# One feed-forward stage of a layer trunk: where VectorE splits the weights of its block products, and where it reads their banks

## The chip, the cores and the metric

The kernel runs on one core of one Trainium2 chip. The metric is the device time of one execution in microseconds; the time of a kernel is the median of its runs. Engines are named as in the profile: PE (TensorE) multiplies, DVE (VectorE) and ACT (ScalarE) work elementwise, POOL (GpSimd) helps and issues some transfers, SP (SyncE) issues the transfers of weights.

## The reference, cut to what matters

Two layers, x of 512 tokens by 1024, in float32. Layer 0 mixes with a recurrent and an RWKV-7 branch, layer 1 with retention; each is followed by a squared-ReLU feed-forward stage, with norms before and after:

```python
def sq_relu_mlp(x, w_in, w_out):
    return jnp.square(jax.nn.relu(x @ w_in)) @ w_out
...
f = sq_relu_mlp(rms_norm(h, norm_ffn_pre[layer]), ffn_w_in[layer], ffn_w_out[layer])
h = h + rms_norm(f, norm_ffn_post[layer])
```

The change lies in the feed-forward stage of layer 1, the last stage: w_in is 1024 by 4096, w_out 4096 by 1024.

## The kernel before, in words

Every product is made of three matmuls in a narrower float format: an operand a is split into a high part (a rounded, written by ACT) and a low part (a minus its high part, written by DVE), and high times high, high times low and low times high are added up in a PSUM bank. Weights come from DRAM in chunks of 128 by 2048 (1 MB) through a ring of three places (`raw`, `WL` over the same bytes, `WH`). SP issues the load of chunk c when PE has begun with chunk c - 2, which shows that it has left c - 3. ACT writes `WH` (L340, or in halves L353 and L354), DVE then writes `WL` (L346, or in halves L359 and L361), and PE waits for `WL` in `chunk_ready`.

The last stage goes over four quarters of the 4096 hidden columns (`ffn_pe`, `ffn_act`, `ffn_dve`). In a quarter whose first chunk is c, eight tiles j = 0 to 7 of hidden activations are computed first, from chunks c to c + 3: PE fills a bank (L388, L391, L394), DVE takes relu (L873) and the square (L881), ACT squares the relu again into the high part AH (L845), DVE subtracts for the low part AL (L884). Chunk c + j/2 + 2 is split by DVE at the end of each even tile (`split_lo`).

In quarters 0, 1 and 2 the second product is computed with seven block products in place of eight (`seven_pe`, `seven_dve`). Of the activations' four blocks four sums are needed (S_both, four steps L747, L748, L750, L752 for each k tile, in `activation_sums`), and of the weights too; the latter were made in an earlier stage and lie in DRAM. Here "sum k" is k tile k of the activations' sums, k = 0 to 3; it is formed behind tile j = 4 + k. Its high part S_high is written by ACT (L708), its low part S_low by DVE (L712, `sums_low`), which stands behind the low part of the next tile, and for sum 3 in `seven_dve`. Product i, i = 0 to 6, uses chunk c + 4 + i and two banks of `SEVEN_BANKS`, each for 128 tokens and 4 k steps: 24 matmuls (L691, L694, L695). Products 0 to 2 use the tiles A themselves, 3 to 6 the sums:

```python
SEVEN_BANKS = ((4, 5), (6, 7), (0, 1), (2, 3), (4, 5), (2, 3), (4, 5))
if t == 0 and i < 2:
    pe.wait_ge(S("a_lo"), done + 4 * i + k + 1)
if t == 0 and i == 3:
    pe.wait_ge(S("sums_lo"), 4 * q + k + 1)
```

So product 1 waits in its k step k for the low part of tile 4 + k, and product 3 for the S_low. DVE adds the two banks of each product into fT (L735, L737), which frees them (`acc_free`). Quarter 3 uses an ordinary product (`out_by_token_pe`), and in quarter 1 PE also turns h by transposes into banks 4 to 7 (L563, `turn_h_pe`), the first of them once banks 4 and 5 are free. POOL loads gain_row (0.5 MB, for the last norm) once the last S_low is written (L1973).

The order of the work is written out by hand: each engine runs its own program, in the order of the loops, and waits on semaphores.

Of the kernel before, what the change touches and what calls it, by code (L numbers as in the profile page):

```python
# [145 lines left out]
def trunk_kernel(nc, x, weights, pairs, vectors, const, ret_const, last_gain, out):  # L146
    with ExitStack() as ctx:
# [5 lines left out]
        def S(name):  # L153
            name = SERIES_OF.get(name, (name,))[0]
            if name not in sems:
                sems[name] = ctx.enter_context(nc.semaphore(name))
            return sems[name]
# [86 lines left out]
        for i in range(2):  # L244
# [5 lines left out]
            q, k = over(f"q{i}", [2, T]), over(f"k{i}", [2, T])  # L250
# [44 lines left out]
        def size(c):  # L295
            return CHUNK // 2 if c in AG_CHUNKS else CHUNK
# [45 lines left out]
        def split_lo(dve, c):  # L342
            if c < ALL_CHUNKS:
                i, n = c % RING, size(c)
                dve.wait_ge(S("w_hi"), c + 1)
                nc.vector.tensor_tensor(WL[i][:, :n], raw[i][:, :n], WH[i][:, :n], ALU.subtract).then_inc(S("w_lo"), 1)  # L346
# [9 lines left out]
        def split_halves_lo(dve, c, n):  # L356
            i, m = c % RING, CHUNK // 2
            dve.wait_ge(S("first_hi"), n + 1)
            nc.vector.tensor_tensor(WL[i][:, :m], raw[i][:, :m], WH[i][:, :m], ALU.subtract)  # L359
            dve.wait_ge(S("w_hi"), c + 1)  # L360
            nc.vector.tensor_tensor(WL[i][:, m:], raw[i][:, m:], WH[i][:, m:], ALU.subtract).then_inc(S("w_lo"), 1)  # L361
# [150 lines left out]
        def post_sum_dve(dve, m, i):  # L512
            dve.wait_ge(S("fsq"), m * KT + 2 * i + 4)
            if i:
                dve.wait_ge(S("fsq_sum_b"), 2 * m + i)
            nc.vector.tensor_tensor(sum_b, sum_b if i else sq[:, 1, :], sq[:, 2 * i + 3, :],
                                    ALU.add).then_inc(S("fsq_sum_b"), 1)
# [28 lines left out]
        def add_to_f(dve, use, b, m, first):  # L546
            n = use.next(b)
            dve.wait_ge(S(f"acc_full{b}"), n)
            if first:
                nc.vector.tensor_copy(f[:, m, :], bank[b][:]).then_inc(S(f"acc_free{b}"), 1)  # L550
            else:
                nc.vector.tensor_tensor(f[:, m, :], f[:, m, :], bank[b][:], ALU.add).then_inc(S(f"acc_free{b}"), 1)  # L552
# [157 lines left out]
        def sums_low(dve, q, k):  # L710
            dve.wait_ge(S("sums_hi"), 4 * q + k + 1)
            nc.vector.tensor_tensor(S_low[:, :, k, :], S_both[:], S_high[:, :, k, :], ALU.subtract).then_inc(S("sums_lo"), 1)  # L712
# [6 lines left out]

        def seven_dve(dve, use, c, q):  # L720
            for i, banks in enumerate(SEVEN_BANKS):
                split_halves_lo(dve, c + 6 + i, 7 * q + i)
                if i == 1:
                    sums_low(dve, q, 3)
                for t, b in enumerate(banks):
                    u = use.next(b)
                    dve.wait_ge(S(f"acc_full{b}"), u)
                    for tokens, outputs, sign in ADDENDS[i]:
                        to = fT[:, 2 * tokens + t, outputs * T:(outputs + 1) * T]
                        last = added.get((tokens, outputs, t))  # L730
                        added[tokens, outputs, t] = b, u
                        if last:
                            dve.wait_ge(S(f"acc_free{last[0]}"), last[1])
                        if not last:
                            ins = nc.vector.tensor_scalar(to, bank[b][:], float(sign), None, ALU.mult)  # L735
                        else:
                            ins = nc.vector.tensor_tensor(to, to, bank[b][:], ALU.add if sign > 0 else ALU.subtract)  # L737
                    ins.then_inc(S(f"acc_free{b}"), 1)

        def activation_sums(dve, q, k):  # L740
            n = 4 * q + k
            dve.wait_ge(S("a_square"), 8 * QUARTERS + 8 * q + 4 + k + 1)
            if n:
                dve.wait_ge(S("sums_lo"), n)
            a11, a21 = first_squared[:, k, 0:HALF], first_squared[:, k, HALF:T]
            a12, a22 = squared[:, k % 2, 0:HALF], squared[:, k % 2, HALF:T]
            nc.vector.tensor_tensor(S_both[:, 0, :], a21, a22, ALU.add).then_inc(S("s_step"), 1)  # L747
            nc.vector.tensor_tensor(S_both[:, 2, :], a11, a21, ALU.subtract).then_inc(S("s_step"), 1)  # L748
            dve.wait_ge(S("s_step"), 4 * n + 1)
            nc.vector.tensor_tensor(S_both[:, 1, :], S_both[:, 0, :], a11, ALU.subtract).then_inc(S("s_step"), 1)  # L750
            dve.wait_ge(S("s_step"), 4 * n + 3)
            nc.vector.tensor_tensor(S_both[:, 3, :], a12, S_both[:, 1, :], ALU.subtract).then_inc(S("s_step"), 1)  # L752
# [35 lines left out]
        def quarter_at(c0, layer, q):  # L788
            return FFN1_AT[q] if layer else c0 + 8 * q
# [71 lines left out]
        def ffn_dve(dve, use, c0, m, layer):  # L861
            dve.wait_ge(S("rb_ready"), m + 1)
            for q in range(QUARTERS):
                done = 8 * QUARTERS * layer + 8 * q
                c = quarter_at(c0, layer, q)
                for j in range(8 if layer else 16):
                    b = j % 4
                    if j < 8:
                        u = use.next(b)
                        dve.wait_ge(S(f"acc_full{b}"), u)  # L870
                        if j >= 2:
                            dve.wait_ge(S("a_lo"), done + j - 1)
                        nc.vector.scalar_tensor_tensor(relu[:, j % 2, :], bank[b][:], 0.0, rB[:], ALU.max,  # L873
                                                       ALU.mult).then_inc(S(f"acc_free{b}"), 1)
                        dve.wait_ge(S(f"acc_free{b}"), u)
                        n, square = T, squared[:, j % 2, :]
                        if layer and q < SEVEN and j < 4:
                            n, square = HALF, first_squared[:, j, :]
                        if layer and q + j // 6:
                            dve.wait_ge(S("s_step"), 16 * min(q, SEVEN) + (4 * (j - 5) if j >= 6 and q < SEVEN else 0))  # L880
                        nc.vector.tensor_tensor(square, relu[:, j % 2, :], relu[:, j % 2, :], ALU.mult).then_inc(S("a_square"), 1)  # L881
                        dve.wait_ge(S("a_square"), done + j + 1)
                        dve.wait_ge(S("a_hi"), done + j + 1)
                        nc.vector.tensor_tensor(AL[:, j, :n], square[:, :n], AH[:, j, :n], ALU.subtract).then_inc(S("a_lo"), 1)  # L884
                        if layer and q < SEVEN and j > 4:
                            sums_low(dve, q, j - 5)
                        if layer and q < SEVEN and j >= 4:
                            activation_sums(dve, q, j - 4)
                    else:
                        add_to_f(dve, use, b, j - 8, q == 0)  # L890
                        if q == QUARTERS - 1 and j in (12, 14):
                            post_sum_dve(dve, m, j // 2 - 6)
                    if j % 2 == 0 and (q or j):
                        split_lo(dve, c + j // 2 + 2)
                    if not layer and q < SEVEN and j in (9, 11, 13, 15):
                        weight_sums_dve(dve, 4 * q + j // 2 - 4)
                if layer and q < SEVEN:
                    seven_dve(dve, use, c, q)
                elif layer:
                    out_by_token_dve(dve, use, c, q)  # L900
# [1146 lines left out]
        def _(dve):  # L2047
# [70 lines left out]
            for m, c0, layer, kind, post, pre in ((1, FFN0_CHUNK, 0, 2, (0, 3), (1, 0)), (2, RET_CHUNK0, 1, 0, (1, 1), (1, 2)),  # L2118
                                                  (3, FFN1_CHUNK, 1, 2, None, None)):
                pre_sums_dve(dve, m)  # L2120
                split_lo(dve, c0 + 2)
                pre_rstd_dve(dve, m)
                if m == 2:
                    ret_dve(dve, use, m)
                else:
                    ffn_dve(dve, use, c0, m, layer)
                if post:
                    residual_dve(dve, m, post, pre)
# [112 lines left out]
```

## Time and profile before

| | |
|---|---|
| median of 3 runs | 1475.59 us (1475.32 to 1476.76) |
| the profiled execution, its own time | 1476.38 us |
| its span | 1474.6 us |
| mean granted clock of PE | 0.986 |
| DVE busy | 921.6 us, 63% |
| ACT busy | 538.2 us, 36% |
| POOL busy | 87.1 us, 6% |
| last stage, quarters 0 to 3 | about 1140 to 1461 us |

The time of an execution is the span and some 2 us around it. A busy share is a mean over all stages; what ends a wait in one stage is read from the rows of that stage. Matmuls are pipelined: each lasts longer than the step from its start to that of the next, so the pace is read from the starts.

### The profile page before, as it was taken

The page shows a single profiled execution, that of the slowest core. Times are in us where ns is not written, and L with a number is a line of the kernel's source. Part 1 is how long each engine was busy: PE and PEld are TensorE (multiplying, and loading weights), DVE is VectorE, ACT ScalarE, POOL GpSimd, SP SyncE. Part 2 cuts the span into 40 slices and gives each one's busy share as a digit, 9 for nine tenths or more (in the row PEclk, how much of TensorE's full clock was granted, in tenths as well). Part 3 has the DMA queues.
Part 4 walks back from the last instruction along what each step waited for, and adds up shares of the span by engine and source line. Part 5 has one row for each costly group of instructions (what it writes and reads, how often), then busy time and mean ns, then how long its engine had stood idle before and what let it go on. Part 6 is the DMA issues. An engine that isn't in the chain of part 4 may idle for free.

```text
span 1474.6 us, 22076 instructions
## 1 busy us (share of the span) xinstructions
PE 1434.8 (97%) x9650; PEld 1181.9 (80%) x9650; DVE 921.6 (63%) x1200; ACT 538.2 (36%) x632; POOL 87.1 (6%) x89
## 2 busy tenths in 40 slices
PE   9999999998999999998999999999998999999997
PEld 6778787777888888887888888888887788888786
DVE  7768676667655565654756445355447876868754
ACT  7555454533312222223343332332434433433322
POOL 0000000012010100001200000000003000000000
PEclk9999999998999999999999999999998999999999
DMA  5211111101474654731222122222130352434332
GB/s 187 73 36 59 50 59 45 59 30 42 178 266 143 224 181 175 263 112 60 86 68 100 62 86 92 81 86 86 62 110 29 132 182 86 171 115 166 134 110 62
DMA packets 30623, 160.21 MB, mean 109 GB/s; under 512 B 2816, under 2 KB 6912, under 8 KB 15552
## 3 DMA queue, kind: packets, MB, share of 16 engines
q1 hardware_dynamic: 23456, 130.73, 25.0%
q0 software_dynamic: 7072, 28.08, 5.4%
q8 instruction: 76, 1.25, 0.3%
q14 instruction: 19, 0.16, 0.0%
HBM read 144.12 MB, written 14.68 MB: 108 GB/s over the span
## 4 chain that ended last, share of the span: by engine, by line
PE 89%; DVE 6%; ACT 2%; issue 1%; DMA 1%; POOL 0%; DVEq 0%; POOLq 0%
PE bank L388 21%; PE bank L394 20%; PE bank L391 20%; PE bank L691 2%; PE bank L695 2%; PE bank L694 2%; PE bank L1681 2%; PE bank L1675 2%; PE bank L1678 2%; PE bank L993 2%; PE bank L402 1%; DMA raw<-weights 1%; PE bank L1000 1%; DVE WL L346 1%; PE bank L593 1%
## 5 line engine op out<-in xcount | busy, mean ns | idle before, releaser
L388 PE MATMUL bank<-XH,WH 128*128 128x512 f32 x944 | 379.4, 402 | 15.4 <-DVE XL L481 12.6
L391 PE MATMUL bank<-XL,WH 128*128 128x512 f32 x944 | 371.2, 393 | 0.0
L394 PE MATMUL bank<-XH,WL 128*128 128x512 f32 x944 | 371.0, 393 | 0.0
L346 DVE TENSOR_TENSOR WL<-raw,WH 128x2048 fp32r<-128x2048 f32 (+1 forms) x99 | 222.1, 2245 | 136.7 <-ACT WH L340 136.6
L340 ACT ACTIVATE WH<-raw 128x2048 fp32r<-128x2048 f32 (+1 forms) x99 | 185.2, 1872 | 189.9 <-DMA raw<-weights 189.8
L388 PEld LDWEIGHTS bank<-XH,WH 128*128 128x128 f32 x944 | 179.5, 190 | 58.8 <-issue 19.5
L394 PEld LDWEIGHTS bank<-XH,WL 128*128 128x128 f32 x944 | 179.4, 190 | 38.7
L391 PEld LDWEIGHTS bank<-XL,WH 128*128 128x128 f32 x944 | 179.7, 190 | 38.2 <-issue 2.1
L845 ACT ACTIVATE AH<-relu 128x512 fp32r<-128x512 f32 (+1 forms) x64 | 37.9, 592 | 216.4 <-DVE relu L873 216.4
L388 PE MATMUL bank<-AH,WH 128*128 128x512 f32 x256 | 99.7, 390 | 0.0
L391 PE MATMUL bank<-AL,WH 128*128 128x512 f32 x256 | 99.6, 389 | 0.0
L394 PE MATMUL bank<-AH,WL 128*128 128x512 f32 x256 | 99.6, 389 | 0.0
L552 DVE TENSOR_TENSOR f<-f,bank 128x512 f32<-128x512 f32 x64 | 43.0, 684 | 67.2 <-PE bank L394 67.0
L873 DVE SCALAR_TENSOR_TENSOR relu<-bank,rB 128x512 f32<-128x512 f32 x64 | 44.0, 688 | 64.9 <-PE bank L394 64.8
L388 PEld LDWEIGHTS bank<-AH,WH 128*128 128x128 f32 x256 | 48.0, 188 | 10.2 <-DVE AL L884 0.3
L394 PEld LDWEIGHTS bank<-AH,WL 128*128 128x128 f32 x256 | 48.0, 188 | 10.0
L391 PEld LDWEIGHTS bank<-AL,WH 128*128 128x128 f32 x256 | 48.0, 188 | 10.0
L388 PE MATMUL bank<-BH,WH 128*128 128x512 f32 x128 | 50.2, 392 | 0.3 <-DVE f L552 0.2
L394 PE MATMUL bank<-BH,WL 128*128 128x512 f32 x128 | 49.8, 389 | 0.0
L391 PE MATMUL bank<-BL,WH 128*128 128x512 f32 x128 | 49.8, 389 | 0.0
L1675 PE MATMUL bank<-WH,XH 128*128 128x512 f32 x128 | 49.8, 389 | 0.0
L1678 PE MATMUL bank<-WL,XH 128*128 128x512 f32 x128 | 49.8, 389 | 0.0
(360 smaller groups left out, 2339.3 us busy)
## 6 DMA issues: line engine op xcount, KB each, us to landing
raw<-weights SPq DMA_DIRECT2D x104, 1024.0 KB, 4.8
block<-weights POOLq DMA_DIRECT2D x12, 1024.0 KB, 7.6
sums_of_blocks<-block POOLq DMA_DIRECT2D x12, 1024.0 KB, 5.3
raw<-sums_of_blocks SPq DMA_DIRECT2D x12, 1024.0 KB, 4.8
raw<-weights SPq DMA_DIRECT2D x8, 512.0 KB, 4.5
h<-x_fm SPq DMA_DIRECT2D x4, 512.0 KB, 8.1
out_tm<-h SPq DMA_DIRECT2D x8, 256.0 KB, 2.6
rc<-ret_const POOLq DMA_DIRECT2D x1, 1536.0 KB, 8.1
```

Of the source, the lines that this page charges most:

```text
L340: nc.scalar.activation(WH[i][:, :n], raw[i][:, :n], ACT.Copy).then_inc(S("w_hi"), 1)
L346: nc.vector.tensor_tensor(WL[i][:, :n], raw[i][:, :n], WH[i][:, :n], ALU.subtract).then_inc(S("w_lo"), 1)
L388: mm = pe.matmul(bank[b][:], wh, xh, start=(k == 0), stop=False)
L391: mm = pe.matmul(bank[b][:], wh, xl, start=False, stop=False)
L394: mm = pe.matmul(bank[b][:], wl, xh, start=False, stop=(k == len(xs) - 1))
L552: nc.vector.tensor_tensor(f[:, m, :], f[:, m, :], bank[b][:], ALU.add).then_inc(S(f"acc_free{b}"), 1)
L691: mm = pe.matmul(bank[b][:], xh, wh, start=(k == 0 and not ADDED[i]), stop=False, skip_group_check=True)
L694: pe.matmul(bank[b][:], xh, wl, start=False, stop=False, skip_group_check=True)
L845: nc.scalar.activation(AH[:, j, :n], relu[:, j % 2, :n], ACT.Square).then_inc(S("a_hi"), 1)
L873: nc.vector.scalar_tensor_tensor(relu[:, j % 2, :], bank[b][:], 0.0, rB[:], ALU.max, ALU.mult).then_inc(S(f"acc_free{b}"), 1)
L1675: mm = pe.matmul(bank[2 + t][:], XH[:, kt, tok], wh, start=(kt == 0), stop=False)
L1678: mm = pe.matmul(bank[2 + t][:], XH[:, kt, tok], wl, start=False, stop=False)
```

## The change

It moves instructions of DVE and changes nothing else. In tile 6 of the last stage's quarters the split of chunk c + 5 (product 1's) is written right behind the tile's low part, ahead of S_low of sum 1 and the steps of sum 2, where it was behind them. In `seven_dve` the two banks of product i are read first, and the split of chunk c + 6 + i (and S_low of sum 3, for i = 1) follows, where the split came first.

```diff
--- before.py
+++ after.py
@@ -719,9 +719,6 @@
 
         def seven_dve(dve, use, c, q):
             for i, banks in enumerate(SEVEN_BANKS):
-                split_halves_lo(dve, c + 6 + i, 7 * q + i)
-                if i == 1:
-                    sums_low(dve, q, 3)
                 for t, b in enumerate(banks):
                     u = use.next(b)
                     dve.wait_ge(S(f"acc_full{b}"), u)
@@ -736,6 +733,9 @@
                         else:
                             ins = nc.vector.tensor_tensor(to, to, bank[b][:], ALU.add if sign > 0 else ALU.subtract)
                     ins.then_inc(S(f"acc_free{b}"), 1)
+                split_halves_lo(dve, c + 6 + i, 7 * q + i)
+                if i == 1:
+                    sums_low(dve, q, 3)
 
         def activation_sums(dve, q, k):
             n = 4 * q + k
@@ -882,6 +882,8 @@
                         dve.wait_ge(S("a_square"), done + j + 1)
                         dve.wait_ge(S("a_hi"), done + j + 1)
                         nc.vector.tensor_tensor(AL[:, j, :n], square[:, :n], AH[:, j, :n], ALU.subtract).then_inc(S("a_lo"), 1)
+                        if layer and j == 6:
+                            split_lo(dve, c + 5)
                         if layer and q < SEVEN and j > 4:
                             sums_low(dve, q, j - 5)
                         if layer and q < SEVEN and j >= 4:
@@ -890,7 +892,7 @@
                         add_to_f(dve, use, b, j - 8, q == 0)
                         if q == QUARTERS - 1 and j in (12, 14):
                             post_sum_dve(dve, m, j // 2 - 6)
-                    if j % 2 == 0 and (q or j):
+                    if j % 2 == 0 and (q or j) and not (layer and j == 6):
                         split_lo(dve, c + j // 2 + 2)
                     if not layer and q < SEVEN and j in (9, 11, 13, 15):
                         weight_sums_dve(dve, 4 * q + j // 2 - 4)
```

DVE's rows of quarter 0 from the low part of tile 6 to the square of tile 7, before. `WL2` is the ring place of product 1's chunk; L747 to L752 are a sum's steps.

```order
L884 TENSOR_TENSOR AL_106<-squared_108,AH_105 128x512
L712 TENSOR_TENSOR S_low_109<-S_both_113,S_high_111 128x4x256
L747 TENSOR_TENSOR S_both_113<-first_squared_112,squared_108 128x256
L748 TENSOR_TENSOR S_both_113<-first_squared_112 128x256
L750 TENSOR_TENSOR S_both_113<-S_both_113,first_squared_112 128x256
L752 TENSOR_TENSOR S_both_113<-squared_108,S_both_113 128x256
L346 TENSOR_TENSOR WL2_57<-raw2_56,WH2_58 128x2048
L873 SCALAR_TENSOR_TENSOR relu_107<-bank2,rB 128x512
L881 TENSOR_TENSOR squared_108<-relu_107 128x512
```

And in the changed kernel:

```order
L884 TENSOR_TENSOR AL_106<-squared_108,AH_105 128x512
L346 TENSOR_TENSOR WL2_57<-raw2_56,WH2_58 128x2048
L712 TENSOR_TENSOR S_low_109<-S_both_113,S_high_111 128x4x256
L747 TENSOR_TENSOR S_both_113<-first_squared_112,squared_108 128x256
L748 TENSOR_TENSOR S_both_113<-first_squared_112 128x256
L750 TENSOR_TENSOR S_both_113<-S_both_113,first_squared_112 128x256
L752 TENSOR_TENSOR S_both_113<-squared_108,S_both_113 128x256
L873 SCALAR_TENSOR_TENSOR relu_107<-bank2,rB 128x512
L881 TENSOR_TENSOR squared_108<-relu_107 128x512
```

The split of product 1's chunk (L346) moved up past S_low and the four steps.

DVE's rows where the seven products of quarter 0 begin, before (the last step of sum 3 stands at the head, and the `x2` rows read the two banks of one product):

```order
L752 TENSOR_TENSOR S_both_113<-squared_108,S_both_113 128x256
L359 TENSOR_TENSOR WL0_51<-raw0_50,WH0_52 128x1024
L361 TENSOR_TENSOR WL0_51<-raw0_50,WH0_52 128x1024
L735 TENSOR_SCALAR fT_49<-bank4 128x512 x2
L359 TENSOR_TENSOR WL1_54<-raw1_53,WH1_55 128x1024
L361 TENSOR_TENSOR WL1_54<-raw1_53,WH1_55 128x1024
L712 TENSOR_TENSOR S_low_109<-S_both_113,S_high_111 128x4x256
L737 TENSOR_TENSOR fT_49<-fT_49,bank6 128x512 x2
```

And in the changed kernel, where L735 and L737 have become L732 and L734:

```order
L752 TENSOR_TENSOR S_both_113<-squared_108,S_both_113 128x256
L732 TENSOR_SCALAR fT_49<-bank4 128x512 x2
L359 TENSOR_TENSOR WL0_51<-raw0_50,WH0_52 128x1024
L361 TENSOR_TENSOR WL0_51<-raw0_50,WH0_52 128x1024
L734 TENSOR_TENSOR fT_49<-fT_49,bank6 128x512 x2
L359 TENSOR_TENSOR WL1_54<-raw1_53,WH1_55 128x1024
L361 TENSOR_TENSOR WL1_54<-raw1_53,WH1_55 128x1024
L712 TENSOR_TENSOR S_low_109<-S_both_113,S_high_111 128x4x256
```

The reads of banks 4 and 5 moved up past the split of product 2's chunk (into `WL0`), those of banks 6 and 7 past the split of product 3's chunk (`WL1`) and S_low of sum 3, and so on with each product.

## Rows read from the trace of the kernel before

**Rows 1.** Page, section 1: busy time (share of the span) and instructions.
```profile
PE 1434.8 (97%) x9650; PEld 1181.9 (80%) x9650; DVE 921.6 (63%) x1200; ACT 538.2 (36%) x632; POOL 87.1 (6%) x89
```

**Rows 2.** Waits, 1120 to 1475 us: engine, line, releaser; total us, times, longest.
```profile
PE bank L691 <- DVE WL L346: 1.9, 1, 1.9
PE bank L691 <- DVE fT L737: 1.2, 1, 1.2
```

**Rows 3.** Order in time, PE, quarter 0, products 0 to 2: start, length, operation [idle before].
```profile
1173.69 0.39 PE L695 MATMUL bank<-WH,AL 128*128 128x512 f32 x1
...
1175.97 0.50 PE L691 MATMUL bank<-WH,AH 128*128 128x512 f32 x1 [1.89 <-DVE WL L346]
...
1178.95 0.63 PE L691 MATMUL bank<-WH,AH 128*128 128x512 f32 x1
...
1183.20 0.40 PE L691 MATMUL bank<-WH,AH 128*128 128x512 f32 x1
```

**Rows 4.** Stretches: length, each engine's busy time, then PE's granted clock, DMA.
```profile
1176.00:1181.40 5.40, 5.40 (x17) 4.24 (x18) 5.18 (x9) 3.13 (x4) 0.00 (x0) 0.68 0.58 194
...
1368.00:1370.00 2.00, 1.89 (x8) 1.61 (x9) 2.00 (x3) 0.46 (x1) 0.00 (x0) 1.00 0.32 41
```

**Rows 5.** Order in time, DVE, quarter 0, tiles 6 and 7 and first splits.
```profile
1168.42 0.68 DVE L873 SCALAR_TENSOR_TENSOR relu<-bank,rB 128x512 f32<-128x512 f32 x1
...
1170.22 0.69 DVE L884 TENSOR_TENSOR AL<-squared,AH 128x512 fp32r<-128x512 f32 x1 [0.39 <-ACT AH L845]
1170.83 1.22 DVE L712 TENSOR_TENSOR S_low<-S_both,S_high 128x1024 fp32r<-128x1024 f32 x1
...
1173.63 2.28 DVE L346 TENSOR_TENSOR WL<-raw,WH 128x2048 fp32r<-128x2048 f32 x1
1175.83 0.68 DVE L873 SCALAR_TENSOR_TENSOR relu<-bank,rB 128x512 f32<-128x512 f32 x1
...
1177.28 0.69 DVE L884 TENSOR_TENSOR AL<-squared,AH 128x512 fp32r<-128x512 f32 x1
...
1180.68 1.22 DVE L359 TENSOR_TENSOR WL<-raw,WH 128x1024 fp32r<-128x1024 f32 x1
1181.82 1.22 DVE L361 TENSOR_TENSOR WL<-raw,WH 128x1024 fp32r<-128x1024 f32 x1
1182.96 1.28 DVE L735 TENSOR_SCALAR fT<-bank 128x512 f32<-128x512 f32 x2
```

**Rows 6.** Order in time, ACT, quarter 0: high half of product 1's chunk.
```profile
1170.03 1.91 ACT L340 ACTIVATE WH<-raw 128x2048 fp32r<-128x2048 f32 x1
```

**Rows 7.** Order in time, quarter 1: PE at products 1 and 2; DVE's split.
```profile
1263.38 0.39 PE L691 MATMUL bank<-WH,AH 128*128 128x512 f32 x1
...
1265.81 1.22 DVE L361 TENSOR_TENSOR WL<-raw,WH 128x1024 fp32r<-128x1024 f32 x1
...
1268.82 0.39 PE L691 MATMUL bank<-WH,AH 128*128 128x512 f32 x1
```

**Rows 8.** Quarter 2: products 2, 5; split, gain_row, chunk's transfer (chain); page's median landing.
```profile
1350.42 0.39 PE L691 MATMUL bank<-WH,AH 128*128 128x512 f32 x1
...
1368.11 0.47 PE L691 MATMUL bank<-WH,S_high 128*128 128x512 f32 x1 [1.21 <-DVE fT L737]
...
1366.15 1.22 DVE L361 TENSOR_TENSOR WL<-raw,WH 128x1024 fp32r<-128x1024 f32 x1
...
1355.12 0.58 POOL L1973 DMA_DIRECT2D gain_row<-last_gain  x1 [219.22 <-DVE S_low L712]
...
1356.28 7.61 DMA raw<-weights
...
raw<-weights SPq DMA_DIRECT2D x104, 1024.0 KB, 4.8
```

**Rows 9.** Order in time, PE, from quarter 0 into quarter 1.
```profile
1215.63 0.39 PE L394 MATMUL bank<-XH,WL 128*128 128x512 f32 x1
1216.20 1.06 PE L563 MATMUL bank<-cst,h 128*128 128x128 f32 x8 [0.18 <-DVE fT L737]
```

## The prediction

> **What bounds the kernel now.** The page's first section comes first: TensorE (PE) is busy for 97% of the span [rows 1]. That figure counts pipelined matmuls, so it says only that PE hardly rests; what a change of VectorE's (DVE's) order can do is read from the places where PE does rest. The waits in the stretch of the second layer's feed-forward stage (1120 to 1475 us) name two of them inside the block products [rows 2]: 1.9 us for the low half of a chunk of weights, and 1.2 us for DVE's reading of a bank.
>
> The order in time shows the first, in quarter 0 [rows 3]. Product 0 issues its last matmul at 1173.69; product 1 begins at 1175.97. A matmul follows the one before after 0.227 us at full clock (24 in the 5.44 us between two products of quarter 1, [rows 7]), so product 1 was due at 1173.92 and begins 2.05 us late. Product 2 begins at 1183.20, 7.23 us later and not 5.44, because the clock fell: the mean granted clock of 1176.0 to 1181.4 is 0.68 [rows 4], which for levels of 1.0 and 0.5 (2.4 and 1.2 GHz) is 3.46 us at the lower one and a loss of 1.73 us. The wait of 1.2 us in quarter 2 has a row of 1.00 behind it [rows 4]; a short wait costs itself alone.
>
> Why was product 1 late? DVE's rows of quarter 0 [rows 5] stand almost end to end: the low part of activation tile 6 (L884 at 1170.22), S_low of sum 1, the four steps of sum 2, the split of product 1's chunk (L346, 1173.63, 2.28 us long), tile 7's relu at 1175.83 and low part at 1177.28, S_low of sum 2, the four steps of sum 3, and at 1180.68 the split of product 2's chunk. That split ends at 1183.04 (L361, 1181.82 plus 1.22), and product 2 starts 0.16 us behind it. So DVE sets both starts in this quarter. In quarter 1 it has slack: the split of product 2's chunk ends at 1265.81 + 1.22 = 1267.03, product 2 starts at 1268.82 [rows 7], and about 0.06 us is the way from a split to PE (1173.63 + 2.28 to 1175.97, rows 3 and 5). The slack is 1.73 us. Quarter 2 repeats quarter 1 81.60 us later (product 2 at 1350.42, [rows 8]).
>
> **Part 1: the split of product 1's chunk goes ahead of sums 1 and 2.** It adds no instruction, but the split needs ScalarE's (ACT's) high half, which ACT writes from 1170.03 to 1171.94 [rows 6]. DVE is ready for it at 1170.83, where S_low starts today. It will stand idle until 1171.97, 1.14 us, while S_low of sum 1 and all behind it queue. Then, in quarter 0:
> - split 1171.97 to 1174.25; product 1 starts at about 1174.32 instead of 1175.97.
> - S_low of sum 1 starts 2.20 us after the split (the step 1173.63 to 1175.83), at 1174.17; S_low and four steps take 2.80 us (1170.83 to 1173.63); relu of tile 7 at about 1176.97, 1.14 us later than now.
> - Tile 7's low part comes 1.45 us after its relu now, 1.80 us at tile 6 (1168.42 to 1170.22), where the relu follows the steps of a sum directly and ACT has S_high to write before the tile's high part. Tile 7 now has tile 6's order, so 0.35 us more: its low part starts at 1178.76, ends at 1179.45, 1.48 us later than now.
> - Product 1 needs tile 7's low part for its fourth k step. Nine matmuls after 1174.32 PE is there at 1176.4 and waits 3.1 us, to 1179.51; that step began at 1178.95 before [rows 3]. The early start is spent within the product.
>
> **Part 2: banks are read before the next split.** Product 0's two bank reads (L735 at 1182.96, 1.28 us long, of which 0.08 lie under the next instruction as with L346) [rows 5] stood behind the split of product 2's chunk and now stand ahead of it. They cost 1.20 us there. With the 1.48 us of part 1 the chunk is late by 2.68 us everywhere, and nothing takes time out of that path, since the instructions are the same.
> - Quarter 0: ready at 1185.72, product 2 at 1185.78 in place of 1183.20: +2.58, and 0.1 for the first matmul after a wait (0.50 against 0.39 long, rows 3 and 7). Product 1 at full clock would end at 1182.9, at the lower one throughout its last 15 by 1.73 later: below 1185.78 either way. So the clock that the old wait cost is no gain here: **+2.7 us**.
> - Quarter 1: 2.68 less the slack of 1.73 makes 0.95, with 0.1 for the restart: **+1.0**.
> - Quarter 2: also +1.0 at product 2, but part of it was lost later already. Product 5 waited 1.21 us (1368.11 in place of 1366.74, that is 1350.42 and three products of 5.44) [rows 8]: DVE could read product 3's banks only behind the split of product 5's chunk, whose transfer took 7.61 us while the load of gain_row, issued at 1355.12, was under way. Now the banks are read first, and the chunk alone counts. Its transfer is issued when product 3 starts, so 1.0 later; the second half of its split, which ended at 1366.15 + 1.22 = 1367.37, ends at 1368.4, and product 5 starts at 1368.5: **+0.4** against 1368.11. Ends: the transfer takes 4.8 us as the page's median does [rows 8], then product 5 starts when PE is there, 1366.74 and 1.0 later, -0.4; the collision is as before, +0.4. I take +0.4, because gain_row's load waits for the last S_low, which moves by the same microsecond.
> - Later products: a product's second bank is full as it ends, 5.44 us after its start, and DVE now waits for that ahead of the next split. The chunk's transfer starts with the same product and takes 4.8 us [rows 8], and then ACT has a first half to write, so the split could hardly begin earlier. No row shows the pair in this order. The bounds are 0 and one read, 0.6 us, which the slack of 1.73 us [rows 7] covers; I take 0.
> - Into quarter 1 the first transposes of h waited for product 6's banks, read behind a split: 1215.63 to 1216.20, 0.57 in place of 0.23 [rows 9]. The reads now come first: **-0.3**. DMA transfers follow the starts of products; none is added. POOL's one wait in the stretch (gain_row) moves as told. In quarter 3 no sum stands behind tile 6, so nothing moves there but the last stage's own order, which is unchanged.
>
> Sum: 2.7 + 1.0 + 0.4 - 0.3 = **+3.8 us**. The profiled execution took 1476.38 (span 1474.6), 0.8 above the median of the runs, 1475.59; against the median this gives **1479.4 us**. By the bounds of these terms the sum lies between 3.0 (the transfer at 4.8) and 4.4 (one read's length uncovered at one place).
>
> **Rivals.**
> A. The clock stays low into product 2 of quarter 0. PE now waits 3.1 us inside product 1 and again in front of product 2; if the lower level covers the start of product 2, its loss of up to 1.73 us [rows 4] is no longer under a wait: +5.4, 1481.0. For it: the wait of 2.05 us brought the lower level. Against it: most of where the lower level could lie is ahead of 1185.78, where PE waits anyway. The Trainium skill (TensorE: Matmul & The Clock Gate, the section HAM oscillation) tells of kernels in which each wait for an operand sends the array back to its lower level, so that every next group starts cold; by that rule A is the forecast and the sum 5.4. The trace bears it out behind the 2.05 us and not behind the 1.21 us wait, so it gets a chance and not the forecast.
> B. The collision on product 5's chunk in quarter 2 goes away: +3.0, 1478.6. For it: product 5 is the only one with such a transfer; against it: both issues move together.
> C. Faster: the early split does what its place says. In quarter 0 product 1 starts 1.65 us earlier, the clock holds, product 2 starts at 1179.9 in place of 1183.20, and the transposes give 0.3: -3.6, 1472.0. It decides at one point: product 2's chunk must be ready by 1183. Against it, DVE's rows [rows 5] leave no pause before 1180.68 to take 2.7 us from.
> D. DVE makes up the lateness in quarters 1 and 2 (the contention of ACT's S_high is smaller, the wait for ACT's high half shorter), so that the slack of 1.73 us covers it: quarter 0 and the transposes alone, +2.4, 1478.0.
> That the change isn't in effect: the rows of the order show both moves in all three quarters, so I give it nothing.
>
> **How the numbers follow.** About 0.2% (2.95 us here) is what can be told from no change. Forecast 0.55, A 0.17, B 0.12, D 0.10, C 0.06. Slower by over 0.2%: the forecast but for 0.05 of it, A, and half of B: 0.73. Within: D, half of B, 0.05: 0.21; faster 0.06. The range takes in B, D and A with 0.6 us of spread between runs: 1477.6 to 1481.7.
>
> **What would show it.** In the profile after: product 1 of quarter 0 starts near 1174.3, with a wait of about 3 us for AL (L884) inside it; product 2 waits for L361 in all three quarters, some 2 to 3 us and twice 1 us; DVE's L346 in quarter 0 to 2 has 1.1 us of idle for ACT ahead of it; no wait of the transposes. I am wrong if product 2 of quarter 1 starts without a wait, or if the time falls.

## The result and the profile after

| | before | changed |
|---|---|---|
| median, 9 runs each | 1475.79 us (1474.83 to 1480.94) | 1479.92 us (1477.40 to 1485.57) |
| ratio | | 1.0027, 95% interval 1.0014 to 1.0039 |
| the profiled execution, its own time | 1476.38 us | 1485.57 us |
| its span | 1474.6 us | 1483.8 us |
| mean granted clock of PE | 0.986 | 0.982 |

The changed kernel is slower by 0.27%: 4.1 us between the two medians, 2.1 to 5.8 us by the interval; 3.8 were forecast. That interval also holds what rivals A, B and D give (+5.4, +3.0, +2.4), so what tells them apart is the trace and not the time. The profiled execution of the changed kernel is the longest of its nine, and much of that has nothing to do with the change: product 0 of quarter 0 starts at 1173.88 there and at 1168.48 before, so 5.4 us were lost ahead of the first instruction that moved. The windows of the changed kernel, and then of the kernel before, over stretches whose code is the same in both (columns as in [rows 4]), show where part of it went:

```profile
40.00:43.00 3.00, 3.00 (x21) 2.13 (x20) 2.86 (x6) 0.00 (x0) 0.00 (x0) 0.63 0.73 300
359.00:368.00 9.00, 9.00 (x34) 7.47 (x34) 2.08 (x3) 0.86 (x2) 0.00 (x0) 0.62 0.00 0
```

```profile
40.00:43.00 3.00, 3.00 (x26) 2.49 (x26) 2.86 (x6) 0.00 (x0) 0.00 (x0) 1.00 0.71 300
359.00:368.00 9.00, 9.00 (x45) 7.50 (x45) 4.42 (x8) 2.13 (x4) 0.00 (x0) 1.00 0.12 26
```

PE was granted 0.63 and 0.62 of its clock where it had 1.00 before, and got 34 matmuls done in 9 us in place of 45. So the two profiles can't be compared by their spans; they are compared from the start of product 0 in each quarter. The waits of PE in the last stage, changed kernel (engine, line, releaser; total us, times, longest):

```profile
PE bank L691 <- DVE WL L361: 2.9, 4, 1.0
PE bank L691 <- DVE AL L884: 2.8, 1, 2.8
PE bank L691 <- DVE WL L346: 0.4, 1, 0.4
```

Against [rows 2] the wait for product 1's chunk (L346) fell from 1.9 to 0.4 us and the wait for a bank read is gone. In their place stand a wait of 2.8 us for a tile's low part (L884) and four waits for the second half of a split (L361). In order of time on PE, changed kernel:

```profile
1179.83 0.50 PE L691 MATMUL bank<-WH,AH 128*128 128x512 f32 x1 [0.35 <-DVE WL L346]
...
1185.03 0.50 PE L691 MATMUL bank<-WH,AH 128*128 128x512 f32 x1 [2.85 <-DVE AL L884]
...
1191.29 0.50 PE L691 MATMUL bank<-WH,AH 128*128 128x512 f32 x1 [0.96 <-DVE WL L361]
...
1224.08 1.03 PE L563 MATMUL bank<-cst,h 128*128 128x128 f32 x8
...
1277.59 0.50 PE L691 MATMUL bank<-WH,AH 128*128 128x512 f32 x1 [0.79 <-DVE WL L361]
...
1360.28 0.50 PE L691 MATMUL bank<-WH,AH 128*128 128x512 f32 x1 [0.79 <-DVE WL L361]
...
1377.29 0.50 PE L691 MATMUL bank<-WH,S_high 128*128 128x512 f32 x1 [0.35 <-DVE WL L361]
```

The first three are quarter 0: product 1 starts 5.95 us after product 0 (7.49 before, [rows 3]), stops in its fourth k step, and product 2 waits again. The fourth row is the first of the transposes, which no longer waits (0.18 us before, [rows 9]). Rows five and six are product 2 of quarters 1 and 2, which did not wait before [rows 7, 8]; the last is product 5 of quarter 2. DVE's rows in quarter 0 answer to [rows 5]:

```profile
1175.74 0.69 DVE L884 TENSOR_TENSOR AL<-squared,AH 128x512 fp32r<-128x512 f32 x1 [0.39 <-ACT AH L845]
1177.48 2.29 DVE L346 TENSOR_TENSOR WL<-raw,WH 128x2048 fp32r<-128x2048 f32 x1 [1.04 <-ACT WH L340]
1179.69 1.22 DVE L712 TENSOR_TENSOR S_low<-S_both,S_high 128x1024 fp32r<-128x1024 f32 x1
...
1182.49 0.68 DVE L873 SCALAR_TENSOR_TENSOR relu<-bank,rB 128x512 f32<-128x512 f32 x1
...
1184.28 0.69 DVE L884 TENSOR_TENSOR AL<-squared,AH 128x512 fp32r<-128x512 f32 x1 [0.38 <-ACT AH L845]
...
1187.69 1.28 DVE L732 TENSOR_SCALAR fT<-bank 128x512 f32<-128x512 f32 x2
1188.89 1.22 DVE L359 TENSOR_TENSOR WL<-raw,WH 128x1024 fp32r<-128x1024 f32 x1
1190.02 1.22 DVE L361 TENSOR_TENSOR WL<-raw,WH 128x1024 fp32r<-128x1024 f32 x1
```

Three terms make product 2 late. DVE stands idle 1.04 us for ACT's high half ahead of the early split (L346), which starts 1.13 us behind the place that S_low had before (0.61 us after the start of the low part, [rows 5]). Tile 7's low part (second L884) waits 0.38 us for ACT and comes 1.79 us behind its relu, where it was 1.45 us. The reads (L732) take 1.20 us ahead of L359. Together 1.13 + 0.34 + 1.20 = 2.67 us; product 2 starts 2.69 us later after product 0 than before.

### The profile page after: what moved, and what is told of

It is laid out like the page before. It is cut to its first block, busy times and chain, and to the rows that moved or that the text cites. A ratio compares the mean times of both kernels' runs of the same rounds, so it can differ in the third digit from the quotient of the medians.

```text
span 1483.8 us, 22076 instructions
## 1 busy us (share of the span) xinstructions
PE 1439.9 (97%) x9650; PEld 1184.7 (80%) x9650; DVE 923.0 (62%) x1200; ACT 538.1 (36%) x632; POOL 87.2 (6%) x89
## 4 chain that ended last, share of the span: by engine, by line
PE 84%; DVE 9%; ACT 3%; issue 2%; POOL 1%; DMA 1%; DVEq 0%; POOLq 0%
PE bank L388 19%; PE bank L394 19%; PE bank L391 19%; PE bank L1680 2%; PE bank L1677 2%; PE bank L1683 2%; PE bank L995 2%; PE bank L691 2%; DVE WL L346 2%; PE bank L694 2%; PE bank L695 2%; PE bank L402 1%; PE bank L1002 1%; ACT WH L340 1%; PE bank L592 1%
## 5 line engine op out<-in xcount | busy, mean ns | idle before, releaser
L346 DVE TENSOR_TENSOR WL<-raw,WH 128x2048 fp32r<-128x2048 f32 (+1 forms) x99 | 222.2, 2246 | 137.4 <-ACT WH L340 137.3
```

## Experiments

Each kernel was traced once, and all runs measure one thing in their traces: the start of products 2, 5 and 6 after the start of product 0 of the same quarter. With a start at every 5.44 us and no wait these would be 10.88, 27.20 and 32.64. "Sum" is the change of the three product 6 figures against before, in us; "T" is the way from product 6 of quarter 0 to product 0 of quarter 1, in which the transposes wait or not; its change is not in the sum.

| kernel | q0: 2, 6 | q1: 2, 6 | q2: 2, 5, 6 | sum | T | ratio (95%) |
|---|---|---|---|---|---|---|
| before | 14.72, 36.50 | 10.88, 32.64 | 10.88, 28.57, 34.10 | | 52.96 | |
| changed | 17.41, 39.31 | 11.83, 33.73 | 11.83, 28.84, 34.42 | +4.2 | 52.57 | 1.0027 (1.0014 to 1.0039) |
| early split alone | 16.17, 38.00 | 10.88, 32.64 | 10.88, 28.41, 33.96 | +1.4 | 52.97 | 1.0002 (0.9987 to 1.0017) |
| reads alone | 15.72, 37.63 | 10.88, 32.64 | 10.88, 27.40, 33.01 | 0.0 | 52.57 | 1.0004 (0.9990 to 1.0019) |
| product 0's reads back | 16.32, 38.11 | 10.88, 32.64 | 10.88, 27.20, 32.64 | +0.2 | 52.57 | 0.9999 (0.9983 to 1.0014) |
| changed, early high half | 16.08, 39.35 | 11.83, 33.74 | 11.83, 29.35, 34.97 | +4.8 | 52.58 | 1.0009 (0.9996 to 1.0022) |
| late reads only | 14.81, 36.65 | 10.88, 32.64 | 10.88, 28.20, 33.77 | -0.2 | 52.57 | 0.9994 (0.9979 to 1.0009) |
| and sums behind tile 7 | 10.88, 35.13 | 10.88, 32.64 | 10.88, 27.53, 33.10 | -2.4 | 52.57 | 0.9988 (0.9972 to 1.0003) |
| late reads, gain_row later | 14.75, 36.62 | 10.88, 32.64 | 10.88, 27.20, 32.64 | -1.3 | 52.57 | 0.9998 (0.9981 to 1.0015) |
| all of the last three, next split first | 10.89, 34.19 | 10.88, 32.64 | 10.88, 27.20, 32.64 | -3.8 | 52.57 | 0.9977 (0.9963 to 0.9990) |

The times of single runs spread by several us, and with them the granted clock (two runs of the kernel before on one chip: 1474.63 us at 0.986, 1484.45 us at 0.979), so the intervals are some 0.3% wide and most experiments are decided by their traces, not by their ratios.

### One part at a time

The early split alone: the hunks of `ffn_dve`, without those of `seven_dve`.

```diff
+                        if layer and j == 6:
+                            split_lo(dve, c + 5)
                         if layer and q < SEVEN and j > 4:
                             sums_low(dve, q, j - 5)
...
-                    if j % 2 == 0 and (q or j):
+                    if j % 2 == 0 and (q or j) and not (layer and j == 6):
                         split_lo(dve, c + j // 2 + 2)
```

> Only the split of product 1's chunk is moved ahead of the sums; banks are read behind the splits as before. Theory (two latenesses on DVE's way to product 2's chunk, 1.48 us from the early split and 1.20 us from the reads, against a slack of 1.73 us in quarters 1 and 2 and none in quarter 0): from the start of product 0 to that of product 2 quarter 0 takes 14.72 + 1.5 = 16.2 to 16.3 us, quarters 1 and 2 stay at 10.88 with no wait, product 5 of quarter 2 still waits 1.4 us for the bank reads; +1.5 us in all (ratio 1.001). Rival 1 (the bank reads alone are the cost, the early split is free): quarter 0 stays at 14.7, time as before. Rival 2 (the early split gains and the reads spoil it): quarter 0 falls to about 11.4, time 3 us below before.

The reads alone: the other way round.

```diff
             for i, banks in enumerate(SEVEN_BANKS):
-                split_halves_lo(dve, c + 6 + i, 7 * q + i)
-                if i == 1:
-                    sums_low(dve, q, 3)
                 for t, b in enumerate(banks):
...
                     ins.then_inc(S(f"acc_free{b}"), 1)
+                split_halves_lo(dve, c + 6 + i, 7 * q + i)
+                if i == 1:
+                    sums_low(dve, q, 3)
```

> Only the bank reads are moved ahead of the splits; the split of product 1's chunk stands behind the sums as before. Theory: product 0 to product 2 takes 14.72 + 1.2 = 15.9 to 16.0 us in quarter 0 and 10.88 in quarters 1 and 2 (1.20 is below the slack of 1.73); product 5 of quarter 2 waits for its chunk alone, 27.8 after product 0 instead of 28.57; the transposes do not wait: +1.2 - 0.75 - 0.35 = +0.1 us (ratio 1.000). Rival 1 (the reads are the cost): 17.4 in quarter 0 and 11.8 in quarters 1 and 2, +3.8 us.

The changed kernel with only product 0's reads back behind the split:

```diff
             for i, banks in enumerate(SEVEN_BANKS):
+                if i == 0:
+                    split_halves_lo(dve, c + 6 + i, 7 * q + i)
                 for t, b in enumerate(banks):
...
-                split_halves_lo(dve, c + 6 + i, 7 * q + i)
+                if i:
+                    split_halves_lo(dve, c + 6 + i, 7 * q + i)
```

> The changed kernel with the reads of product 0's two banks put back behind the split of product 2's chunk; the other products' reads stay ahead. Theory: as with the early split alone up to product 2 (16.2 to 16.3 us in quarter 0, 10.88 and no wait in quarters 1 and 2), then product 5 of quarter 2 at 27.8 after product 0 and no wait of the transposes: +1.5 - 0.75 - 0.35 = +0.4 us. Rival 1 (all reads cost, at every product): waits at products 3 to 6 too, +2 us or more. Rival 2 (the early split alone brings the waits in quarters 1 and 2): 11.8 there, +2.4.

Product 2 of quarter 0 came at 16.17, 15.72 and 16.32, within 0.3 us of what the theory gave (16.2 to 16.3, 15.9 to 16.0, 16.2 to 16.3). In quarters 1 and 2 all three stay at 10.88 without a wait. Both rivals fall: neither part alone brings the waits of the changed kernel there, and the early split alone does not make quarter 0 shorter. The delays themselves can be read in quarter 1, from the second half of the split of product 2's chunk. It started 7.87 us after product 0 (1257.94) before [rows 7]. The same row with the early split alone:

```profile
1271.49 1.22 DVE L361 TENSOR_TENSOR WL<-raw,WH 128x1024 fp32r<-128x1024 f32 x1
```

With the reads alone:

```profile
1269.51 1.22 DVE L361 TENSOR_TENSOR WL<-raw,WH 128x1024 fp32r<-128x1024 f32 x1
```

And in the changed kernel:

```profile
1276.32 1.22 DVE L361 TENSOR_TENSOR WL<-raw,WH 128x1024 fp32r<-128x1024 f32 x1
```

Product 0 of quarter 1 starts at 1262.13, 1260.42 and 1265.76 in these three, so the split is late by 1.49, 1.22 and 2.69 us. That is the point of the case: 1.49 and 1.22 us each fit under the slack of 1.73 us, and their sum does not; what is left over, 0.96 us, is the 0.95 us by which product 2 is late. The parts add up to +1.4 and 0.0 us by their traces; together they cost +4.2. Of the 2.8 us between, 1.1 are quarter 1's and 1.6 quarter 2's, where the length of one transfer plays a part too.

What the early split does in quarter 0 is seen in its own trace, the waits of PE inside the last stage's products, with the split alone:

```profile
PE bank L691 <- DVE AL L884: 2.9, 1, 2.9
PE bank L691 <- DVE fT L737: 1.1, 1, 1.1
PE bank L691 <- DVE WL L346: 0.2, 1, 0.2
```

The 1.9 us for L346 became 2.9 us for L884 inside the same product. Two sizes in quarter 2 were missed: product 5 came at 27.40 and 27.20 where 27.8 was expected. Its chunk took 7.2 and 5.2 us from issue to ACT's first half in these two runs, and 7.6 before; the last but one experiment shows what makes that transfer long.

### The wait for ACT

The changed kernel, with ACT's high half of product 1's chunk written earlier in quarter 0:

```diff
+                    if layer and q == 0 and j == 6:
+                        split_hi(act, c + 5)
                     if layer and q < SEVEN and j > 4:
                         sums_high(act, q, j - 5)
...
-                    if j % 2 == 0 and (q or j):
+                    if j % 2 == 0 and (q or j) and not (layer and q == 0 and j == 6):
                         split_hi(act, c + j // 2 + 2)
```

> The changed kernel, but in quarter 0 ACT writes the high half of product 1's chunk ahead of S_high of sum 1 and tile 6's high part, so that DVE need not wait for it. Theory: DVE's idle 1.04 us ahead of that split in quarter 0 goes, product 1 starts on time, and product 0 to product 2 takes 17.41 - 1.1 = 16.3 us there; quarters 1 and 2 as in the changed kernel (11.83); 1.1 us below the changed kernel. Rival (the wait for ACT does not count, DVE's own amount of work does): quarter 0 stays at 17.4.

DVE, order in time, in this kernel:

```profile
1170.05 0.69 DVE L886 TENSOR_TENSOR AL<-squared,AH 128x512 fp32r<-128x512 f32 x1 [0.39 <-ACT AH L847]
1170.66 2.29 DVE L346 TENSOR_TENSOR WL<-raw,WH 128x2048 fp32r<-128x2048 f32 x1
```

The idle time ahead of the split is gone, and product 2 starts at 16.08 in place of 17.41, 1.3 us earlier (1.1 expected). So the wait for ACT was a term of its own. (A wait is given here as the time by which a start comes later than 0.227 us after the start before it; the idle time in the rows is some 0.16 us less.) But product 3 comes at 23.03, as late as the 22.99 of the changed kernel. Windows of this kernel, product 2 from 1184.46 on:

```profile
1178.00:1184.00 6.00, 3.74 (x15) 2.74 (x15) 5.86 (x10) 4.20 (x5) 0.00 (x0) 1.00 0.06 23
1184.00:1188.00 4.00, 3.54 (x9) 2.83 (x10) 4.00 (x6) 0.00 (x0) 0.00 (x0) 0.57 0.39 125
1188.00:1191.50 3.50, 3.50 (x17) 2.90 (x16) 1.61 (x2) 1.44 (x2) 0.00 (x0) 1.00 0.39 162
```

Behind the first of two waits (2.33 us late) the clock stays at 1.00; behind the second (2.68 us late) it is 0.57 over 1184 to 1188, where product 2 runs: 6.95 us for it in place of 5.44. That is rival A of the prediction, in an execution of another kernel. In the changed kernel's own trace the lower level lies inside product 1, ahead of product 2's wait, where it costs nothing:

```profile
1185.00:1189.30 4.30, 4.27 (x12) 3.36 (x13) 4.16 (x8) 2.58 (x4) 0.00 (x0) 0.60 0.00 0
1189.30:1191.30 2.00, 1.04 (x6) 0.52 (x4) 2.00 (x3) 1.46 (x2) 0.00 (x0) 1.00 0.00 0
1191.30:1197.00 5.70, 5.70 (x25) 4.73 (x26) 5.14 (x6) 0.35 (x1) 0.00 (x0) 1.00 0.52 187
```

In quarter 0 PE stands idle 1.8 us or more at the start of product 1 or inside it in eight of the traces here; in seven of them the lower level lies inside product 1, and only in the run with the early high half in product 2. How often it falls on the one side or the other in executions of the changed kernel was not measured. The ratio of the early high half, 1.0009 (up to 1.0022), is lower than its trace's +4.4 us (0.3%) would make it, so that execution was probably one of the worse ones; at 1480.70 us it is the second longest of ten.

### What a gain is made of

The kernel before, with the reads of products 2 to 6 alone moved:

```diff
             for i, banks in enumerate(SEVEN_BANKS):
-                split_halves_lo(dve, c + 6 + i, 7 * q + i)
+                if i < 2:
+                    split_halves_lo(dve, c + 6 + i, 7 * q + i)
                 if i == 1:
                     sums_low(dve, q, 3)
...
                     ins.then_inc(S(f"acc_free{b}"), 1)
+                if i >= 2:
+                    split_halves_lo(dve, c + 6 + i, 7 * q + i)
```

> The kernel before, with the bank reads of products 2 to 6 alone moved ahead of the splits; the split of product 1's chunk and the reads of products 0 and 1 stay where they were. Theory: nothing stands on DVE's way to product 2's chunk, so product 0 to product 2 takes 14.7 us in quarter 0 and 10.88 in quarters 1 and 2, as before; the gains of the moved reads remain: the transposes do not wait (-0.35), and product 5 of quarter 2 waits for its chunk alone or not at all (27.2 to 27.9 after product 0 instead of 28.57): -1.0 to -1.7 us (ratio 0.999). Rival (the reads gain nothing, what was seen there were shorter transfers): 28.4 to 28.6, time as before.

Quarter 0 and 1 as expected, T shorter by 0.39; but product 5 of quarter 2 came at 28.20, outside the range. Its chunk took 8.0 us from issue (1357.45) to ACT's first half (1365.40), 0.3 more than before. That is also short of the rival's 28.4 to 28.6: what product 5 waits for is now the chunk itself (L361) and no longer a bank read, which came 0.74 us behind the chunk before (1367.37 to 1368.11, [rows 8]). So the reads do gain there, by an estimate from these rows some 0.7 us, and the longer transfer took about half of it back. The next run but one moves gain_row's load away from it. First the order of quarter 0, on top of the late reads:

```diff
-                        if layer and q < SEVEN and j > 4:
-                            sums_low(dve, q, j - 5)
-                        if layer and q < SEVEN and j >= 4:
-                            activation_sums(dve, q, j - 4)
+                        if layer and q == 0 and j >= 6:
+                            if j == 7:
+                                split_halves_lo(dve, c + 6, 0)
+                                sums_low(dve, q, 1)
+                                activation_sums(dve, q, 2)
+                                split_halves_lo(dve, c + 7, 1)
+                                sums_low(dve, q, 2)
+                                activation_sums(dve, q, 3)
...
```

(with ACT's high half early, its S_high of sums 2 and 3 behind the high halves of the chunks of products 2 and 3, and `seven_dve` leaving out those two splits in quarter 0.)

> As the run before, and in quarter 0 the early split without what it held up: ACT writes the chunk's high half ahead of S_high of sum 1, DVE splits product 1's chunk right behind tile 6, and S_low of sum 1 and sums 2 and 3 stand behind tile 7 and the split of product 2's chunk. Theory: product 1 of quarter 0 starts on time with no wait inside it, product 2 on time (10.9 after product 0), the clock holds, and product 3 waits about 1 us for S_low of sum 3: product 0 to product 6 takes 33.7 us in place of 36.5; with the gains of the run before -4.0 to -4.6 us (ratio 0.997). Rival (DVE's amount of work ahead of product 2 sets the time, whatever its order): product 2 or 3 as late as before, 36 us or more.

Products 1 and 2 of quarter 0 start on time, though DVE has the same instructions, so not their amount held product 2 but the order, DVE's and with it ACT's, which this run changes too. Product 3 waited 1.06 us as expected, but product 4 another 1.13 for its own chunk, whose split now stood behind six bank reads: 35.13 where 33.7 was expected, and with the transposes -2.8 us in place of -4.0 to -4.6.

Then gain_row's load, on top of the late reads alone:

```diff
                     pool.wait_ge(S("sums_lo"), 4 * SEVEN)
+                    pool.wait_ge(S("a_lo"), 8 * QUARTERS + 8 * SEVEN + 1)
                     pool.dma_start(gain_row[:], last_gain).then_inc(S("gain_loaded"), 16)
```

> The kernel with the reads of products 2 to 6 ahead of the splits (everything else as before), and POOL's load of gain_row held back until quarter 3's first tile is done. Theory (product 5's wait in quarter 2 is that its chunk's transfer runs beside gain_row's load): the transfer takes 4.8 us like the others, product 5 starts 27.2 after product 0 and product 6 at 32.6, quarter 0 as before with its wait of 2 us; -1.5 and -0.35 for the transposes: -1.8 us (ratio 0.999). Rival (the transfer is long for another reason, such as its place in memory): still 7 us or more, product 5 at 27.8 or later.

```profile
1355.23 0.33 SPq L1944 DMA_DIRECT2D raw<-weights  x1
...
1360.07 1.06 ACT L353 ACTIVATE WH<-raw 128x1024 fp32r<-128x1024 f32 x1 [3.41 <-DMA raw<-weights]
...
1384.93 0.58 POOL L1977 DMA_DIRECT2D gain_row<-last_gain  x1 [249.84 <-DVE AL L887]
```

SP issues the chunk's load at 1355.23, and ACT has it at 1360.07, 4.84 us later; gain_row's load comes at 1384.93. Product 5 starts at 27.20, with no wait in quarter 2. So it was gain_row's load that held the chunk, and not its place in memory. At last all of these, with the split of product 4's chunk ahead of the reads of products 1 and 2:

```diff
                 if i == 1:
                     sums_low(dve, q, 3)
+                    if q == 0:
+                        split_halves_lo(dve, c + 8, 2)
...
-                if i >= 2:
+                if i >= 2 and (q or i > 2):
                     split_halves_lo(dve, c + 6 + i, 7 * q + i)
```

> The order with sums 2 and 3 behind tile 7 in quarter 0, where product 4 had waited 1.1 us for its chunk: now the split of product 4's chunk stands ahead of the bank reads of products 1 and 2, and gain_row's load comes later as in the run before. Theory: in quarter 0 products 1 and 2 start on time, product 3 waits 1.0 us inside for S_low of sum 3, product 4 no longer waits (21.8 + 1.1 = 22.9 after product 0), product 6 at 33.8 in place of 36.5; quarters 1 and 2 at 32.6 without waits; in all -2.7 - 1.5 - 0.35 = -4.5 us against before (ratio 0.997). Rival (the load on DVE ahead of product 4 sets its start whatever the order): product 4 at 24 again, -3.2 us.

PE's only wait in the last stage's products:

```profile
PE bank L691 <- DVE S_low L714: 1.2, 1, 1.2
```

Product 4 follows product 3 without a wait, so the place of its chunk's split on DVE was what held it; product 3's own wait grew from 1.06 to 1.36 us, and product 6 of quarter 0 comes at 34.19 (33.8 expected). The sum is -3.8, and with -0.39 for the transposes -4.2 us, where -4.5 was expected. The time is 0.9977 of before, interval 0.9963 to 0.9990: 1474.33 against 1477.74 us on that chip. The changed kernel, at 1.0027 of before, was not run beside it. The four edits together are clear of the noise; by its ratio none of the steps to it is.

## Why the prediction was right

- Sign, size and place held: 1479.4 forecast, 1479.92 measured; +3.8 forecast, +3.8 in the trace (4.2 in the products, -0.39 at the transposes).
- Part 1. DVE's wait for ACT was to put the split 1.14 us behind S_low's old place; it came 1.13 us behind it, 1.04 of them idle. Tile 7's low part was to come 0.35 us later after its relu; it came 0.34 later. Product 1 was to start 0.4 late and then to wait 3.1 us for tile 7; it was 0.51 late, and the wait made the step 3.01 us late.
- Part 2. The reads' 1.20 us are the step from 1187.69 to 1188.89. Product 2 of quarter 0 was to start 2.58 us later and starts 2.69 later; with the slower first matmul +2.7 was forecast, and product 3 is 22.99 - 20.18 = 2.81 later. Quarter 1 was put at +1.0 and has +1.09 at product 6. The term for later products was put at 0: products 3 to 6 of quarters 0 and 1 follow each other at 5.44 us. The transposes were put at -0.3, they are -0.39.
- Quarter 2 was put at +0.4 and is +0.32, but that closeness is in part luck: the term hangs on one transfer. The kernel with the early high half has the same code in quarter 2, its chunk took 8.0 us from issue to ACT in place of 7.5, and it has +0.87.
- The slack of 1.73 us, read from one row of quarter 1, carried the forecast for two quarters. The runs show it from both sides: nothing happens at delays of 1.49 and 1.22 us, and 2.69 us makes product 2 late by 0.95. Rival D fell with it: the wait for ACT's high half is 1.04 us in all three quarters of the changed kernel.
- One reading was wrong without harm. DVE was said to set the start of product 2 in quarter 0 before. PE has no wait there [rows 3]: product 1's lower clock brought it to product 2 0.16 us behind the chunk, 0.10 more than the way to PE takes. Both limits lay within 0.1 us of each other, so the sum did not suffer.
- Rival A was not what the changed kernel's trace shows, but the run with the early high half shows that it occurs, and that the argument against it was too quick. Fifteen matmuls at the lower level were given a loss of 1.73 us at most; that is the loss of a stretch of 3.46 us. At the lower level's step of 0.43 us (1186.38 to 1186.80 in the changed kernel) all fifteen would take 6.4 us and end at about 1185.9, not ahead of 1185.78. In the trace at hand some eight of them ran at that pace, and the loss stayed hidden ahead of product 2's chunk; that need not be so in each execution. It shortened PE's wait for that chunk, which was to be 2 to 3 us and is 0.96.
- The Trainium skill (TensorE: Matmul & The Clock Gate, HAM oscillation) tells of a kernel in which each wait for an operand sends the array back to its lower level. The traces here agree behind the waits of 3.0 us (0.60) and 2.7 us (0.57). They do not behind the 2.33 us of the run with the early high half (1.00) nor behind the 0.95 us of quarters 1 and 2. So in this kernel not each wait does it, and the rows decide where the lower level costs.
- Rival B (the collision in quarter 2 goes away) did not come with the change: the chunk's transfer takes 7.44 us after, 7.61 before [rows 8]. It came with product 0's reads put back, whose chunk was issued 0.06 us behind gain_row's load (1357.18 and 1357.12) instead of 1.2 us: 5.2 us to ACT.
- Rival C fell for the reason given: with the split early and sums 1 and 2 behind it, tile 7 and product 2's chunk are late. It needed the sums behind tile 7 as well, as the last runs show.

## What to carry to other kernels

Moving an instruction ahead on an engine that runs its program in order, as DVE does here (it stood idle 1.04 us while S_low was queued), moves its own wait ahead too: look at when its input is ready, and put what the wait would hold up either in front of it or so far behind that nobody asks for it yet. Two delays that are each covered by the same slack must be added before they are compared with it. When a wait on the bounding engine is taken away, look for the next thing that same stretch of work needs; here that was tile 7's low part, nine matmuls into the product.

## What the runs showed of the hardware

- A 1 MB load took 4.8 and 5.0 us from its issue to ACT's first half in the two runs that held gain_row's load back. It took 7.2 to 8.0 us in the seven traces (before, changed, five experiments) in which POOL's 0.5 MB load had been issued 1.1 to 1.2 us before it, and 5.2 us where that was issued 0.06 us before it; the 0.5 MB load then took 6.1 us to land, in place of 3.5 to 3.6. What sets its length between 7.2 and 8.0 us was not found.
- The granted clock of stretches with the same code differed between two executions (0.62 against 1.00 over 9 us near 360 us, where PE had been idle for 0.57 us, up to 358.23, in the slower one alone); such stretches gave a part of the 5.4 us by which the two differed ahead of the change. Over 40 to 43 us it was 0.63 and 1.00 behind the same idle of PE, 1.67 us, which ended at 37.64 and 37.74. So of two like waits one brought the lower level and the other did not.
- A profile's span is a poor measure of a change of 0.3%. Distances between instructions inside the stage, where no wait, transfer or lower clock differs, repeated to 0.1 us: without a wait quarter 1 took 32.64 us to product 6 in all eight such traces, and T was 52.57 or 52.58 in eight.
